# Gate sums spread through memory, values reversed by their stationary rows, and one weight rest made earlier

## What is computed

```python
proj = rms_norm(x, norm_g[l]) @ w_in[l]
q_a, k_a, v_a, q_h, f_h, i_h, q_m, z = jnp.split(proj, split_points, axis=-1)
o_h = hgrn2_chunkwise(q_h, f_h, i_h, lb_all[l])      # i_h: the values
y = jnp.concatenate([o_a, o_h, o_m], axis=-1) * jax.nn.silu(z)
x = x + y @ w_out[l]
```

```python
g = -jnp.exp(dn_A_log) * jax.nn.softplus(dn_a + dn_dt_bias)
G = jnp.cumsum(g, axis=-1)                           # in each chunk
decay = jnp.where(causal, jnp.exp(G[..., :, None] - G[..., None, :]), 0.0)
y = (gt[:, :, 0] * (o_dn @ w_branch_dn) + gt[:, :, 1] * (o_pool @ w_branch_pool)
     + gt[:, :, 2] * (o_ret @ w_branch_ret))
```

## Time and profile before

| | |
|---|---|
| time, median of three runs | 1340.68 us (1340.37 to 1341.74) |
| time of the profiled execution | 1340.78 us |
| its span | 1339.0 us |
| PE, PEld busy | 1323.3 us (99%), 1132.6 us (85%) |
| DVE, ACT, POOL busy | 934.2 (70%), 740.5 (55%), 97.5 us (7%) |
| DMA | 227.67 MB, mean 170 GB/s |

### The profile page before, as it was taken

The page is one execution under the profiler, slowest core; times in us unless marked ns, Lnnn a source line. Parts: engine busy times, 40 slices in busy tenths (PEclk is TensorE's granted clock), DMA queues, the critical chain, the costliest instruction groups (busy, mean ns, idle before and its releaser), DMA issues.

```text
span 1339.0 us, 17869 instructions
## 1 busy us (share of the span) xinstructions
PE 1323.3 (99%) x7049; PEld 1132.6 (85%) x7049; DVE 934.2 (70%) x1238; ACT 740.5 (55%) x1057; POOL 97.5 (7%) x126
## 2 busy tenths in 40 slices
PE   9999999999999999999999999999999999999998
PEld 7988888978888899888878888889988887888886
DVE  6789876699876497786885555466696778655544
ACT  6864775675684466444465444456754445544432
POOL 1002000001200001500000000000123000000000
PEclk9999999999999999999999999999999999999999
DMA  8654335455236355644464565635564445466552
GB/s 285 219 179 154 98 126 183 164 172 174 95 126 222 107 196 181 191 157 142 157 221 127 188 189 173 232 134 185 185 188 157 157 142 189 156 189 188 189 182 101
DMA packets 140291, 227.67 MB, mean 170 GB/s; under 512 B 8400, under 2 KB 55312, under 8 KB 139952
## 3 DMA queue, kind: packets, MB, share of 16 engines
q1 hardware_dynamic: 137968, 221.67, 50.5%
q0 software_dynamic: 576, 2.23, 1.0%
q10 hardware_dynamic: 1664, 2.63, 0.5%
HBM read 225.33 MB, written 1.18 MB: 169 GB/s over the span
## 4 chain that ended last, share of the span: by engine, by line
PE 91%; DVE 5%; ACT 2%; issue 1%; POOL 1%; DMA 1%; SPq 0%; ACTq 0%; DVEq 0%
PE gp L694 70%; PE gp L682 9%; PE mp L662 4%; DVE arena L1591 2%; PE mp L1007 2%; DVE wt_rest L1597 1%; PE mp L823 1%; PE mp L890 1%; POOL rs_out L2411 1%; PE mp L865 1%; PE mp L844 1%; PE mp L851 1%; ACT first_hi L1194 1%; DMA wt<-in_w_mem_kv 1%; DVE small L2147 0%
## 5 line engine op out<-in xcount | busy, mean ns | idle before, releaser
L1597 DVE TENSOR_TENSOR wt_rest<-wt,wt_hi 128x1024 fp32r<-128x1024 f32 x148 | 174.5, 1221 | 80.8 <-ACT wt_hi L1194 78.8
L1194 ACT ACTIVATE mix_hi<-wt 128x1024 fp32r<-128x1024 f32 x128 | 132.5, 1059 | 129.3 <-PE gp L694 99.2
L1194 ACT ACTIVATE wt_hi<-wt 128x1024 fp32r<-128x1024 f32 x148 | 148.0, 1053 | 95.3 <-DMA wt<-in_ffn_down 48.6
L1597 DVE TENSOR_TENSOR wt_rest<-wt,mix_hi 128x1024 fp32r<-128x1024 f32 x128 | 151.9, 1230 | 46.7 <-ACT mix_hi L1194 46.0
L1597 DVE TENSOR_TENSOR wt_rest<-wt,first_hi 128x1024 fp32r<-128x1024 f32 x104 | 124.0, 1221 | 26.0 <-ACT first_hi L1194 25.1
L2411 POOL TENSOR_TENSOR rs_out<-rs_in,minus_half 128x1 f32<-128x1 f32 (+3 forms) x35 | 54.0, 1544 | 1178.0 <-DVE rs_in L1602 1178.0
L694 PE MATMUL gp<-mix_hi,mix_hT_hi 128*128 128x512 f32 x320 | 127.0, 397 | 0.9 <-DVE wt_rest L1597 0.9
L694 PE MATMUL gp<-wt_hi,hT_hi 128*128 128x512 f32 x320 | 126.8, 396 | 0.0
L1194 ACT ACTIVATE first_hi<-wt 128x1024 fp32r<-128x1024 f32 x104 | 105.7, 1059 | 36.9 <-PE gp L694 26.1
L694 PE MATMUL gp<-wt_hi,hT_rest 128*128 128x512 f32 x320 | 125.0, 391 | 0.0
L694 PE MATMUL gp<-wt_rest,mix_hT_hi 128*128 128x512 f32 x320 | 124.8, 390 | 0.0
(11 more groups left out here) (347 smaller groups left out, 2991.4 us busy)
## 6 DMA issues: line engine op xcount, KB each, us to landing
wt<-in_w_in SPq DMA_DIRECT2D x96, 1024.0 KB, 5.1
wt<-in_w_out SPq DMA_DIRECT2D x20, 1024.0 KB, 5.1
wt<-in_ffn_gate SPq DMA_DIRECT2D x40, 512.0 KB, 4.0
wt<-in_ffn_up SPq DMA_DIRECT2D x40, 512.0 KB, 5.0
wt<-in_ffn_down SPq DMA_DIRECT2D x20, 1024.0 KB, 5.1
wt<-in_w_mem_kv SPq DMA_DIRECT2D x7, 1024.0 KB, 5.2
arena<-in_w_in SPq DMA_DIRECT2D x4, 1024.0 KB, 8.2
wt<-in_w_branch_pool SPq DMA_DIRECT2D x4, 1024.0 KB, 5.0
```

The costliest lines, as they stand in the source:

```text
L1194: nc.scalar.activation(rounded_part(u)[:, k:k + nk, :], raw_of(u)[:, k:k + nk, :], ACT.Copy)\
L1597: return nc.vector.tensor_tensor(o, i0, i1, ALU.subtract)
```

## The change

Three things change, in both layers of their block.

1. Gates. `gbc`, `gb0` and `gb1` go. VectorE copies the summed gates out of `cg`; after K's second unit TensorE transposes them (step `cgT`, two transposes of 128 x 4); VectorE copies the four rows of 256 out, those of tile 1 reversed; GpSimd writes them to memory, waits, and reads them back with one DMA that gives every partition all 1024 numbers (`gate_sums`, `spread_gates`). VectorE's order is now: `rests_until(9)`, the copies of `cgT`, `convolve(1)`, the wait for that DMA, the two differences and `decay`, then `rests_until(11)`.
2. Values. `ihr` goes. While TensorE works on FH and QH, GpSimd copies the split rows of tile 1 with the tokens reversed (`turn_rows`), and IH's product for tile 1 uses these as its stationary rows. TensorE waits for the copies before IH.
3. A rest. `rests_until(29)` now stands at the end of the inverse's last level, ahead of `gate_pool(0)`.

```diff
-ORDER_1 = ... + ["hg1", "hg2", "ihr"] + [f"hg{n}" for n in range(3, 8)] \
+ORDER_1 = ... + ["hg1", "hg2"] + [f"hg{n}" for n in range(3, 8)] \
...
-ORDER_2 = ... + ["ba", "bat", "cg", "gb0", "gb1"] \
+ORDER_2 = ... + ["ba", "bat", "cg", "cgT"] \
...
+            if group in SPLIT_A and n == "IH" and t == 1:
+                return back_hi[:, k, :], back_rest[:, k, :]
...
-                for g in ("QH", "IH"):
-                    split_units(s(g), 2)
+                split_units(s("QH"), 2)
+                pe.wait_ge(sig("rows_turned"), 2 * (l + 1))
+                split_units(s("IH"), 2)
...
-                    end(nc.tensor.matmul(bank(s("ihr")), flip, reg("A", "IH")[:, 1, :], start=True, stop=True))
...
-                for t in range(TT):
-                    begin(s(f"gb{t}"), (sig("gates_ready"), l + 1))
-                    for h in range(NH):
-                        last = nc.tensor.matmul(bank(s(f"gb{t}"))[:, P * h:P * h + P], gbc[:, NH * t + h, :], upper if t == 0 else lower[:, ::-1], start=True, stop=True)
-                    end(last)
                 split_units(s("K"), 1)
+                begin(s("cgT"), (sig("gates_summed"), l + 1))
+                for t in range(TT):
+                    last = nc.tensor.transpose(bank(s("cgT"))[0:4, P * t:P * t + P], small[:, 56 + 4 * t:60 + 4 * t], ident)
+                end(last)
...
-                    if n == 3:
-                        evacuate("ihr", reg("A", "IH")[:, 1, :], bank(s("ihr")))
...
-                nc.scalar.activation(eg, bank(s("gb1"), NH, P), ACT.Exp).then_inc(step_read[STEP_NO[s("gb1")] % 4], 1)
+                nc.scalar.activation(eg, gate_sums[:, 1], ACT.Exp).then_inc(sig("gate_exp"), 1)
...
-                copy(gbc, gates[:, :, None].to_broadcast([P, 8, P])).then_inc(sig("gates_ready"), 1)
...
                 dve.wait_ge(*computed(s("cg")))
-                v(copy(small[:, 56:64], bank(s("cg"))[:, 0:8]))
+                copy(small[:, 56:64], bank(s("cg"))[:, 0:8]).then_inc(sig("gates_summed"), 1)
+                dve.wait_ge(sig("gates_summed"), l + 1)
                 evac(sub(small[:, 64:72], bank(s("cg"))[:, 8:16], small[:, 56:64]), s("cg"))
-                dve.wait_ge(*computed(s("gb0")))
-                evac(sub(decay[:, 0], bank(s("gb0"), NH, P), over(small[:, 56:60], NH, P)), s("gb0"))
-                dve.wait_ge(*computed(s("gb1")))
-                v(sub(decay[:, 1], bank(s("gb1"), NH, P), over(small[:, 60:64], NH, P)))
+                rests_until(9)
+                dve.wait_ge(*computed(s("cgT")))
+                copy(ba_rows[0:4, 0:P], bank(s("cgT"))[0:4, 0:P])
+                evac(copy(ba_rows[0:4, P:S], bank(s("cgT"))[0:4, S - 1:P - 1:-1]), s("cgT"))
+                gates_after[len(pow_widths)] = l
+                convolve(1)
+                dve.wait_ge(sig("gates_spread"), 16 * (l + 1))
+                sub(decay[:, 0], gate_sums[:, 0], over(small[:, 56:60], NH, P))
+                v(sub(decay[:, 1], gate_sums[:, 1], over(small[:, 60:64], NH, P)))
                 nc.vector.scalar_tensor_tensor(decay, decay, -1.0, decay, ALU.mult, ALU.min).then_inc(sig("decay_in"), 1)
-                rests_until(9)
-                convolve(1)
                 rests_until(11)
...
                         for t in range(TT):
                             mul(invT[:, t], both_inv, over_heads(upper_lower[:, t])).then_inc(sig("inverse"), 1)
+                        rests_until(29)
...
+            def spread_gates(l):
+                pool.wait_ge(*read_out(f"B{l}.cgT"))
+                pool.dma_start(gates_out[l].rearrange("t h c -> h t c"), ba_rows[0:4].rearrange("h (t c) -> h t c", t=TT)).then_inc(sig("gates_written"), 16)
+                pool.wait_ge(sig("gates_written"), 16 * (l + 1))
+                pool.dma_start(gate_sums.rearrange("p t h c -> p (t h c)"),
+                               gates_out[l].rearrange("(o t) h c -> o (t h c)", o=1).to_broadcast([P, TT * NH * P])).then_inc(sig("gates_spread"), 16)
+
+            def turn_rows(l):
+                pool.wait_ge(sig("first_split"), TT * (l + 1))
+                pool.wait_ge(*summed(f"A{l}.VM"))
+                for dst, src in ((back_hi, first_hT_hi), (back_rest, first_hT_rest)):
+                    nc.gpsimd.tensor_copy(dst[:, :, :], src[:, 1, :, ::-1].bitcast(F)).then_inc(sig("rows_turned"), 1)
             for n, (at, width) in enumerate(pow_widths):
+                if n in turn_after:
+                    turn_rows(turn_after[n])
+                if n in gates_after:
+                    spread_gates(gates_after[n])
```

More of the change, by code:

```diff
@@ L116 @@
 COL_B_ROWS = TAP_ROWS + DEPTH * (NH + 4)
-ORDER_1 = [f"xT{i}" for i in range(4)] + ["kmT0", "kmT1"] + ["hg1", "hg2", "ihr"] + [f"hg{n}" for n in range(3, 8)] \
+ORDER_1 = [f"xT{i}" for i in range(4)] + ["kmT0", "kmT1"] + ["hg1", "hg2"] + [f"hg{n}" for n in range(3, 8)] \
     + ["hg0_0", "hg0_1", "hg8", "qmT0", "qmT1"] + [f"ms{h}" for h in range(4)] + [f"mpt{h}" for h in range(4)] + ["qaT0", "qaT1", "kaT0", "kaT1"] \
@@ L122 @@
     + [f"pt{h}" for h in range(8)] + ["oa0", "oa1", "yT0", "yT1"]
-ORDER_2 = [f"xT{i}" for i in range(4)] + ["ba", "bat", "cg", "gb0", "gb1"] \
+ORDER_2 = [f"xT{i}" for i in range(4)] + ["ba", "bat", "cg", "cgT"] \
     + [f"bT{j}{t}" for j in range(3) for t in range(2)] \
@@ L334, in mixer_program @@
         both_inv, turned_inv, left_inv, yl = (region(b_e + 1024 + 512 * i, NH, P) for i in range(4))
-        gbc = region(b_ml, 8, P)
+        gate_sums = region(b_ml, TT, NH, P)
         ba_rows = region(b_e + 2048, S)
@@ L386, in mixer_program @@
         first_hT_hi = part("first_hT_hi", R1["QH"], TT, KD, P)
+        back_hi, back_rest = part("back_hi", a_PT, KD, P), part("back_rest", a_PT + KD * P, KD, P)
         final_hi = part("final_hi", R1["QH"], UNIT_K, F32_COLS)
@@ L438, in mixer_program @@
         pow_widths = []
-        inverse_after = {}
+        inverse_after, gates_after, turn_after = {}, {}, {}
+        gates_out = nc.dram_tensor("gates_out", (DEPTH, TT, NH, P), F, kind="Internal").ap()
         rows_out = nc.dram_tensor("rows_out", (DEPTH, P, 2 * NH * EDGE), F, kind="Internal").ap()
@@ L834, in hg_diagonals @@
                     hg_quad(s("hg0_1"), lambda h: ks_back[:, h, :], lambda h: qs[:, h, S - 1:P - 1:-1])
-                def flip_values():
-                    begin(s("ihr"), (loaded["flips"], 16))
-                    pe.wait_ge(group_read[GROUP_NO[s("IH")] % 2], GROUP_NO[s("IH")] // 2 + 1)
-                    end(nc.tensor.matmul(bank(s("ihr")), flip, reg("A", "IH")[:, 1, :], start=True, stop=True))
                 def scores(h):
@@ L870, in hg_values @@
                     for t in range(TT):
-                        begin(s(f"hgo{t}"), read_out(s("hg0_0")), read_out(s("hg0_1")), read_out(s("hg8")), read_out(s("ihr")))
+                        begin(s(f"hgo{t}"), read_out(s("hg0_0")), read_out(s("hg0_1")), read_out(s("hg8")), taken(s("IH")))
                         for h in range(NH):
@@ L901, in y_taken @@
                         pe.wait_ge(*read_out(s(f"yT{2 * j + t}")))
[L902 to L905, removed]
                 def query_transposes():
@@ L911, in _ @@
                 for n, g in enumerate(("QM", "QA", "QA", "KA", "KA", "VA", "VA")):
-                    split_units(s(g), 1, halfway=lambda: level_and_values(n + 1))
+                    split_units(s(g), 1, halfway=lambda: hg_level(n + 1))
                 hg_diagonals()
@@ L975, in _ @@
                 end(nc.tensor.matmul(bank(s("cg"))[:, 8:16], ones, gcol, start=True, stop=True))
+                split_units(s("K"), 1)
+                begin(s("cgT"), (sig("gates_summed"), l + 1))
                 for t in range(TT):
-                    begin(s(f"gb{t}"), (sig("gates_ready"), l + 1))
-                    for h in range(NH):
-                        last = nc.tensor.matmul(bank(s(f"gb{t}"))[:, P * h:P * h + P], gbc[:, NH * t + h, :], upper if t == 0 else lower[:, ::-1], start=True, stop=True)
-                    end(last)
-                split_units(s("K"), 1)
+                    last = nc.tensor.transpose(bank(s("cgT"))[0:4, P * t:P * t + P], small[:, 56 + 4 * t:60 + 4 * t], ident)
+                end(last)
                 split_units(s("V"), 2)
@@ L1784, in _ @@
                 mul(km, km, over(given(asked), 8, P)).then_inc(sig("km_normed"), 1)
+                turn_after[len(pow_widths)] = l
                 if l == 0:
@@ L2124, in _ @@
                 v(nc.vector.scalar_tensor_tensor(gates, small[:, 104:112], 0.0, small[:, 40:48], ALU.max, ALU.add))
-                v(nc.vector.scalar_tensor_tensor(gates2, gates2, -1.0, small[:, 48:52][:, None, :].to_broadcast([P, 2, 4]), ALU.mult, ALU.mult))
-                copy(gbc, gates[:, :, None].to_broadcast([P, 8, P])).then_inc(sig("gates_ready"), 1)
+                nc.vector.scalar_tensor_tensor(gates2, gates2, -1.0, small[:, 48:52][:, None, :].to_broadcast([P, 2, 4]), ALU.mult, ALU.mult)\
+                    .then_inc(sig("gates_ready"), 1)
```

(3 more changed lines are left out.)

## The result

The changed kernel takes 1342.76 us (median of 22 runs, 1341.34 to 1346.87) against 1340.62 for the kernel before: a ratio of 1.0017, 95% interval 1.0011 to 1.0024. It is 2.1 us slower, inside 0.2%, where the forecast of 1339.3 was 1.5 us faster: 3.5 us lie between the two. The profiled execution took 1342.72 us, span 1340.9.

The account below looks back on a forecast made before the run. TensorE, busy 99% of the 1339.0 us span, was taken to bound the kernel. Per layer L - 3.2 - 0.89 - 1.67, for two 2L - 11.5, -1.5 us with L = 5.0: 1339.3 us from 1340.78; 8-in-10 range 1335.2 to 1343.3.

Parts of the forecast that it names:

- so the shift stays: Behind RV's start: VectorE's work keeps its distances from TensorE, so RV's shift of L - 3.2 us a layer persists.
- the gates' travel: Mixer block: gate sums go through memory instead of TensorE products; L - 3.2 us a layer, where 1.79 was to be saved.
- the reversal: First block: reversal product leaves TensorE between level 2 and level 3; 0.89 us won a layer.
- the moved rest: Mixer block: BP1's rests made ahead of the gating end TensorE's idle time before BP1; 1.67 us won a layer.
- L: Time from issue to landing of GpSimd's 512 KB read of the gate sums; taken as 5.0 us.
- unobstructed rival: Gate read gets its packets out before the weight load: L = 3.0, time 1335.3 us; chance 0.37.
- Write to read: GpSimd's gate transfer: 2.59 us from issue of the write to issue of the read.
- My stall, L - 2.2: TensorE idle ahead of RV by L - 2.2 us, 2.8 with L = 5.0.
- wait for the sums ahead of the transposes: After K's second unit TensorE idles about 0.5 us for the summed gates before the small transposes.
- the zero for what pays for it: First block: GpSimd's reversal copies and TensorE's wait for them ahead of IH were counted as costing zero.
- my bound: First block: GpSimd's two reversal copies take 22.4 us at its dearest rate, inside some 24 us available.
- The queued read: Gate read queues behind the weight load: L = 8.1, VectorE idle, RV 4.9 us late, time 1345.5; chance 0.14.

Follow-up runs that it names:

- x9: Changed kernel with 34 unread transposes on TensorE between V and RV in the second layer, filling the stall: 1340.72 us, ratio 1.0001.
- x12: Kernel before, no transfer added, VectorE repeating an idle copy nine times per layer ahead of RV's rests: 1355.76 us, ratio 1.0111.
- x6: Changed kernel with SyncE waiting for the gate sums before it issues the weight load beside the read: 1338.19 us, ratio 0.9986.
- x13: Changed kernel with SyncE holding two weight loads, beside the write and beside the read, until the gate sums land: 1339.30 us, ratio 0.9989.
- x7: Changed kernel with VectorE's two small copies ahead of the rests of V's second unit, so the write is issued earlier: 1342.66 us, ratio 1.0014.
- x3: Kernel before with only the reversal by GpSimd copies: 1339.99 us, ratio 0.9993.
- x4: Kernel before with only the moved pooled-branch rest: 1336.72 us, ratio 0.9971.
- x10: Kernel before, no transfer added, VectorE repeating an idle copy five times per layer ahead of RV's rests: 1346.28 us, ratio 1.0040.

## Why the prediction was wrong

**The step that failed is "so the shift stays".** The prediction took the later start of RV for the whole cost: behind it TensorE was to run as before, so its idle time was priced one for one, and the clock stood at nothing in the sum. But RV itself took 13.74 us in the second layer, 2.6 more than behind a stall at full clock (11.15). x9 gave most of that back without an earlier read, and x12 brought it on without any read. Over the 22 runs the mean granted clock goes with the time: 0.998 in the nine shortest (1341.3 to 1342.1 us), 0.994 in the longest (1346.87). With the 2.6 us taken off, the profile would be at 1340.1, 0.7 us below the one before: an estimate, but the sign would be the forecast one.

The 3.4 us between forecast and profile add up from the table of landmarks: half clock +2.6, the gates' travel +0.6 (4.2 against 3.6), the reversal +0.7 (1.07 won against 1.78), the moved rest -0.5 (3.8 won against 3.3).

**L was right in the mean and wrong in its spread.** I took 5.0 for both layers; it was 4.27 (482.98 to 487.25) and 5.68 (935.15 to 940.83), mean 4.98. I had put the weight load half a microsecond behind the read; it is so in the first layer and the other way round in the second. That matters because the second stall, and not the mean, pays for the clock. The unobstructed rival was out of reach: with no weight load issued beside it (x6, x13) the read still took 3.7 to 4.1 us, not 3.0, nor the 3.2 estimated with it in the prediction (3.0 against 2.3 for the fastest small read was no close agreement either).

**Write to read was mis-sized in one layer.** I took 2.59; it was 2.19 and 3.58, the second because the write waits for a weight load under way (x7, x13). The Trainium skill ("DMA: Bandwidth & Descriptors", Queues, rings and completion order) has a DMA engine take turns between its queues by packets; by that alone the 4 KB of the write would land soon beside a load. These runs show it late: 1.8 us alone (x13), 3.7 and 4.8 when issued into a load (x7), so the taking of turns does not price it. Why the write waits that long no run here shows.

**The rest of the chain held.** My stall, L - 2.2 corrected by the write step, is 4.27 - 2.2 - 0.40 = 1.7 and 5.68 - 2.2 + 0.99 = 4.5 us; measured 1.56 and 4.33. The wait for the sums ahead of the transposes was 0.3 us each, predicted 0.5. Both layers' gates cost 0.47 + 3.23 + 2 x 0.24 = 4.2 us without the clock, predicted 2 x 5.0 - 6.4 = 3.6.

**The reversal gave 1.07 us, not 1.78.** The step itself was right: level 2 to level 3 is now 299.23 - 292.89 = 6.34 us, against 7.24. What failed is the zero for what pays for it. GpSimd's copies are far under my bound. In the second layer they take 1.35 and 1.05 us:

```profile
242.56 1.35 POOL L2419 CAST back_hi<-first_hT_hi 128x1024 fp32r<-128x1024 f32 x1 [0.81 <-PE gp L698]
243.85 1.05 POOL L2419 CAST back_rest<-first_hT_rest 128x1024 fp32r<-128x1024 f32 x1
```

But they hold up VectorE, which works beside them in both layers. The first layer, GpSimd and VectorE in the changed kernel, then VectorE before:

```profile
40.24 2.04 POOL L2419 CAST back_rest<-first_hT_rest 128x1024 fp32r<-128x1024 f32 x1
...
39.33 2.04 DVE L1584 TENSOR_TENSOR arena<-arena,rs_out 128x1024 f32<-128x1024 f32 x1 [0.39 <-POOL rs_out L2428]
41.30 1.00 DVE L1670 TENSOR_SCALAR small<-pos 128x2 f32<-128x2 int32 x1
```

```profile
39.70 1.22 DVE L1591 TENSOR_TENSOR arena<-arena,rs_out 128x1024 f32<-128x1024 f32 x1 [0.39 <-POOL rs_out L2411]
40.84 0.16 DVE L1677 TENSOR_SCALAR small<-pos 128x2 f32<-128x2 int32 x1
```

These two instructions of VectorE take 2.04 to 2.06 and 1.00 to 1.01 us in all ten traces with the copies, 1.22 to 1.23 and 0.16 in all six without. VectorE's next rests start at 45.66 instead of 44.37, and TensorE needs 43.44 us from the start of FH to level 1 (34.51 to 77.95) where it needed 42.97 (34.77 to 77.74): 0.47 lost. That the one comes from the other is read off the traces; no run tests it alone. In the second layer VectorE is held up too (1.00 us for an instruction of 0.16, 2.01 for a rest of 1.2), but there it costs TensorE nothing near by: level 3 comes 6.34 us behind level 2. Further on the query transposes now wait 0.37 us for VectorE, where before nothing waited; what makes VectorE late there is open (timeline of TensorE).

```profile
334.63 0.55 PE L666 MATMUL mp<-const,arena 128*128 128x128 f32 x3 [0.37 <-DVE arena L1883]
```

The 1.07 also holds 0.26 us won ahead of FH (34.51 against 34.77), where the start of an execution scatters: FH starts anywhere from 34.12 to 34.77 in the six traces without the copies and from 34.14 to 35.85 in the ten with them. From FH to the landmark the six need 419.49 to 419.61 us and the ten 418.41 to 418.94, so the reversal is worth 0.8 us in the mean, near x3's 0.7.

**The moved rest** was right and a little too small: 1.67 us of idle time is 1.9 with the restart behind it; x4 measured 3.95 for two.

**The rivals.** The queued read came nearest: VectorE idle, RV late. But an L of 5.7 in one layer was enough for a loss of 2.1 us where I wanted 7.1 in both for one of 2.7, since the clock added its price.

## What to carry to other kernels

Idle time of a busy TensorE is not priced one for one. One stall of 4.3 us cost more here (4.33 + 0.24 + 2.59 = 7.2 us) than three of 1.6 would (3 x 1.8), so look at the longest stall that an uncertain transfer can make, not at the mean over its places. When work behind a new wait does not need what is waited for, move it ahead: one line on VectorE turned a loss of 2.1 us into a gain of 4.9. Holding competing loads back can move the lateness to their own users, as two held loads did here. And a copy given to an engine that is free is not free while another engine runs beside it: look at the neighbour's instructions too.

## What was unexpected of the hardware

- The granted clock fell to half behind stalls of 3.5 us and more in all seven cases, and behind two of three of 2.01 to 2.05 us; of two stalls that differ by 0.02 us in one execution (x10) one cost 1.6 us more. The Trainium skill ("TensorE: Matmul & The Clock Gate", Part 1) has the clock go between these two levels with how busy TensorE was, and these runs agree.
- A restart at full clock costs 0.24 us beyond the idle time.
- The fall is dearer behind stalls of 4.3 us (13.5 to 13.9 for RV) than behind 3.5 (12.8) or 5.0 (13.1 to 13.5). RV runs longer at half clock there (5.5 us against 3.4 and 4.1 to 4.9); what sets that length the profile does not settle.
- A write of 4 KB from GpSimd's queue took 1.8 us alone and up to 4.8 when issued into a weight load of another queue.
- GpSimd's copies and VectorE's work hold each other up: 2.04 us for GpSimd's copy of 128x1024 against 1.04 to 1.05, 2.04 for VectorE's 128x1024 multiplication against 1.22, 1.00 for a 128x2 instruction against 0.16. Each time 0.8 to 1.0 us is added, so the rows look as if one of two waited while the other ran; no run here tests that.
